# Loading each expert weight as two 1 MB transfers, awaited and released by halves

## The chip, the cores and the metric

The kernel runs on one core of one Trainium2 chip. The metric is the time of one execution on the device in microseconds (us), taken as the median of several runs. Before the change it is 1430.96 us (three runs, 1430.59 to 1434.89).

## What is computed

A decoder trunk of two layers over 256 tokens of width 1024, all in float32. Layer 0 mixes tokens by attention, layer 1 by a gated delta rule (GDN). After each mixer stands a layer norm, then a mixture of experts (MoE), then another layer norm:

```python
for layer in range(2):
    mix = attention_mixer(...) if layer % 2 == 0 else gdn_mixer(...)
    x = layer_norm(DEEPNORM_ALPHA * x + mix, ...)
    ffn = moe_ffn(x, router_w, router_bias, moe_w1[layer], moe_w3[layer], moe_w2[layer])
    x = layer_norm(DEEPNORM_ALPHA * x + ffn, ...)

def expert_block(xb, e):                      # inside moe_ffn
    hb = jax.nn.silu(xb @ w1[e]) * (xb @ w3[e])
    return hb @ w2[e]
```

Each token goes to the best 2 experts of one group of 8 out of 32. w1 and w3 of an expert are 1024 x 512, w2 is 512 x 1024: three matrices of 2 MB each, 6 MB per expert, 32 experts per layer, 384 MB for both layers.

## The kernel before, in words

The kernel loads the weights of every expert of both layers, whatever the routing is. The order of the work is written out by hand, engine by engine, with semaphores between them; there is no planner.

**The weight slots.** Nine slots of 2 MB each hold weights (`slot_tile`, L263): six in `ring` and three in a work area called `arena`. Attention and GDN use the ring slots for their own projection weights. In the MoE the nine slots hold three experts, and matrix m of expert n takes the slot `slot_moe(layer, 3 * n + m)` (L103): m = 0 is w1, 1 is w3, 2 is w2. The slots repeat every three experts.

**The loads.** All of them are issued by SyncE (SP) on its one hardware queue, in program order, by `load_expert` at L444 to L448. SP waits until a slot is free, then issues one transfer of 2 MB for it. For the first three experts of a layer `first_free` says what must be over (`free_for_moe0`, `free_for_moe1`: points of the attention or the GDN). From the fourth expert on, `freed` waits for PE to have finished the same matrix of the expert three before: `w1_used` for w1, `h_ps` for w3, `y_ps` for w2. Of w1 and w3 each of the 128 partitions gets one run of 16 KB, of w2 it gets two runs of 8 KB (`expert_parts`, `part`). After the last expert SP reads a flag (`load_more`), which sends nothing more when no expert has over 32 tokens, and then issues the GDN weights (`load_gdn`, L439, runs of 2 KB).

**TensorE** works through the experts in `experts` (L788; `turn` is one trip of three). For one expert: wait for w1, 64 matmul instructions at L803; wait for w3, 64 more; add the previous expert's output to the sum over experts (`scatter`, L784); transpose the gated product (L809); gather the next expert's tokens (`gather`, L763 and L766); wait for w2, 32 instructions at L817; transpose the next tokens (L774). The last instruction on a matrix raises the semaphore that frees its slot. ScalarE and VectorE run the gating between w3 and w2 and copy results out of PSUM. After the last expert PE runs one more `scatter`, and VectorE the layer norm.

**After `moe(0)`** PE goes on with the GDN; after `moe(1)` the final layer norm and the store of the output end the kernel.

Of the kernel before, what the change touches and what calls it, by code (L numbers as in the profile page):

```python
# [52 lines left out]
NE = 32  # L53
# [136 lines left out]
def build(nc, a, out):  # L190
    with ExitStack() as ctx:
# [3 lines left out]
        def sem(name):  # L195
            return ctx.enter_context(nc.semaphore(name))
# [118 lines left out]
        def gates_of(shape):  # L315
# [26 lines left out]
        ident_in, const_in, small_in, ln_in, gdn_in, out_done = (  # L342
            sem(n) for n in ("ident_in", "const_in", "small_in", "ln_in", "gdn_in", "out_done"))
        slot_full = [sem(f"slot_full{i}") for i in range(SLOTS)]
        x_half = [sem(f"x_half{t}") for t in range(NT)]
        first_in = [sem(f"first_in{i}") for i in range(2)]
        init = sem("init")
# [51 lines left out]
        def moe_sems(name):  # L399
            return [sem(f"{name}_{s}") for s in ("pick", "gathered", "xe", "gpt", "w1_used", "h_ps", "sig", "hm", "hT_ps",  # L400
                                                 "hT", "y_ps", "y", "own", "scattered")]

        fast_sems = moe_sems("moe")
        fast = [Moe(fast_sems), Moe(fast_sems, 1, NE)]
        more = [Moe(moe_sems("more0")), Moe(moe_sems("more1"))]
        more_full = [[sem(f"more{layer}_full{i}") for i in range(RING)] for layer in range(2)]

        block = ctx.enter_context(nc.Block())
# [21 lines left out]
        def _(sp):  # L430
            def part(m, slot):
                dst = slot_tile(slot)
                return dst.rearrange("p (h q) n -> p h (q n)", h=2) if m == 2 else dst

            def load_att(u, src):
                sp.dma_start(ring[:, slot_att(u)], src).then_inc(slot_full[slot_att(u)], 16)

# [3 lines left out]
            def load_experts(layer, first_free):  # L441
                s = fast[layer]

                def load_expert(e, c, wait):  # L444
                    for m, src in enumerate(expert_parts(layer, e)):
                        wait(m)
                        slot = slot_moe(layer, 3 * c + m)
                        sp.dma_start(part(m, slot), src).then_inc(slot_full[slot], 16)  # L448

                def freed(n):  # L450
                    def wait(m):
                        sp.wait_ge((s.w1_used, s.h_ps, s.y_ps)[m], n + (s.e + 1 - DEPTH))
                    return wait

                for n in range(DEPTH):
                    load_expert(n, n, lambda m: first_free(3 * n + m))
                for n in range(DEPTH, GROUP):
                    load_expert(n, n, freed(n))
                with sp.Fori(1, NE // GROUP) as i:
                    for c in range(GROUP):  # L460
                        load_expert(i * GROUP + c, c, freed(i * GROUP + c))
                for n in range(NE // GROUP * GROUP, NE):
                    load_expert(n, n % GROUP, freed(n))

            def load_more(layer):

                s = more[layer]
                sp.wait_ge(flag_sb, layer + 1)
                over = sp.value_load(flag[0:1, layer, 0:1])
                with sp.If(over > CAP):  # L470
                    sp.wait_ge(fast[layer].y_ps, NE + fast[layer].e)

                    def load_expert(n, c, again=True):
                        for m, src in enumerate(expert_parts(layer, n % NE)):
                            if again:
                                sp.wait_ge((s.w1_used, s.h_ps, s.y_ps)[m], n + (s.e + 1 - DEPTH))
                            sp.dma_start(part(m, 3 * c + m), src).then_inc(more_full[layer][2 * c + m // 2], 16)

                    for n in range(DEPTH):
                        load_expert(n, n, False)  # L480
                    with sp.Fori(1, (NIT - NE) // DEPTH) as i:
                        for c in range(DEPTH):
                            load_expert(i * DEPTH + c, c)
                    for n in range((NIT - NE) // DEPTH * DEPTH, NIT - NE):
                        load_expert(n, n % DEPTH)
                    sp.wait_ge(s.y_ps, NIT - NE)
                with sp.Else():
                    sp.nop()

# [102 lines left out]
        def _(pe):  # L592
# [192 lines left out]
                                  skip_group_check=not (stop and t == NT - 1), tile_position=(h * CAP, 0))  # L785
                return last

            def experts(s, steps, slot_of, full):  # L788

                def turn(i, cs, ends):  # L790
                    for c in cs:
                        n, b = i * GROUP + c, c % GROUP
                        ends_here = ends and c == cs[-1]
                        slots = [slot_of(3 * c + m) for m in range(3)]
                        filled = [full(i, c, m) for m in range(3)]
                        pe.wait_ge(s.xe, i * (2 * GROUP) + (2 * c + 2 + 2 * s.e))
                        pe.wait_ge(s.gpt, n + (2 + s.g))

                        for m in range(2):
                            pe.wait_ge(*filled[m])  # L800
                            for j in range(DJ):
                                for h in range(TILES):
                                    last = mm(psum[5][h * CAP:(h + 1) * CAP, m * FH:(m + 1) * FH], xeT[:, j],  # L803
                                              slot_tile(slots[m])[:, j, h // 2 * SEQ + h % 2:(h // 2 + 1) * SEQ:2],
                                              start=(j == 0), stop=(j == DJ - 1), tile_position=(0, h * CAP))
                            last.then_inc((s.w1_used, s.h_ps)[m], 1)
                        scatter(s, (b - 1) % GROUP, n + 1)
                        pe.wait_ge(s.hm, n + (1 + s.e))
                        transpose(psum[6][:, 0:P], hm, ident).then_inc(s.hT_ps, 1)  # L809
                        if not ends_here:  # L810
                            gather(s, (b + 1) % GROUP, n + 2)
                        pe.wait_ge(s.hT, n + (1 + s.e))
                        pe.wait_ge(*filled[2])
                        w2 = w2_view(slots[2])
                        for g in range(TILES):
                            for h in range(TILES):
                                last = mm(psum[7][h * CAP:(h + 1) * CAP, 0:Q], hT[:, g],  # L817
                                          w2[:, g // 2, g % 2, h * Q:(h + 1) * Q],
                                          start=(g == 0), stop=(g == TILES - 1), tile_position=(0, h * CAP))
                        last.then_inc(s.y_ps, 1)  # L820
                        if not ends_here:
                            turn_tokens(s, i * (2 * GROUP) + (2 * c + 3 + 2 * s.e))

                gather(s, 0, 1)
                turn_tokens(s, 1 + 2 * s.e)
                whole = (steps - 1) // GROUP
                with pe.Fori(0, whole) as i:
                    turn(i, range(GROUP), False)
                turn(whole, range(steps - whole * GROUP), True)
                scatter(s, (steps - 1) % GROUP, steps + 1, True).then_inc(s.scattered, 1)  # L830

            def moe(layer):
                router(layer)
                def full(i, c, m):
                    slot = slot_moe(layer, 3 * c + m)
                    return slot_full[slot], i * 16 + 16 * (MOE_BASE[layer][slot] + 1)

                def more_ready(i, c, m):
                    each = 16 if m == 2 else 32
                    return more_full[layer][2 * c + m // 2], i * each + each  # L840

                experts(fast[layer], NE, lambda u: slot_moe(layer, u), full)
                pe.wait_ge(flag_sb, layer + 1)
                over = pe.value_load(flag[0:1, layer, 0:1])
                with pe.If(over > CAP):
                    pe.wait_ge(more[layer].y, 1)
                    for h in range(TILES):
                        mm(psum[h][:], ident, y[:, :, h * Q:(h + 1) * Q], start=True, stop=False)
                    experts(more[layer], NIT - NE, lambda u: u, more_ready)
                with pe.Else():  # L850
                    pe.nop()
                pe.sem_inc(mix_ps, 4)
# [520 lines left out]
        def _(dve):  # L1373
# [268 lines left out]
            def moe(layer):  # L1642
# [4 lines left out]
                with dve.If(over > CAP):  # L1647
                    dve.wait_ge(fast[layer].scattered, 1 + fast[layer].runs)
                    experts(layer, more[layer], NIT - NE, NE)
                    dve.wait_ge(more[layer].scattered, 1)  # L1650
                with dve.Else():
                    dve.wait_ge(fast[layer].scattered, 1 + fast[layer].runs)
                layer_norm(1 + 2 * layer)
# [222 lines left out]
```

## Time and profile before

| what | value |
|---|---|
| median of 3 runs | 1430.96 us |
| the profiled execution's own time | 1432.51 us |
| its span, first to last instruction | 1430.6 us |
| mean granted TensorE clock | 0.945 |
| PE busy | 1161.7 us (81%) |
| DVE / ACT / POOL busy | 28% / 16% / 1% |
| DMA | 461.20 MB, mean 322 GB/s over the span |

Busy shares count instructions alone. The DMA share of a stretch is the mean over the core's 16 DMA engines of the time that their packets took; successive packets on an engine overlap by a few ns, so it can read a little over 1. A packet is one contiguous run, or the few bytes that raise a semaphore. Times are from the start of the span. "PE bank L803 <- DMA" in the waits means that a matmul at L803 stood still until a transfer landed.

### The profile page before, as it was taken

To read this page: it belongs to the slowest core of one execution; us is meant where nothing else is said; L and a number is where in the kernel's file an instruction comes from. 1 tells how busy PE (TensorE), PEld (TensorE's weight loads), DVE (VectorE), ACT (ScalarE), POOL (GpSimd) and SP (SyncE) were. 2 spreads that over 40 slices of the span, in tenths; PEclk is the share of its full clock that TensorE was granted. 3 is DMA by queue.
4 is the path that set the end of the run, shared out by engine and by line. 5 is a ranking of instruction groups with operands and counts; after the bars stand their busy time and mean duration, and the time that the engine had idled before them with its cause. 6 is when DMAs were issued, how large, how long until landed. Compare 5 with 4: busy or idle time off the path is not lost. (4 is left out here: it accounts for less than half of the span.)

```text
span 1430.6 us, 34064 instructions
## 1 busy us (share of the span) xinstructions
PE 1161.7 (81%) x14947; PEld 732.3 (51%) x14947; DVE 399.6 (28%) x1126; ACT 224.4 (16%) x589; POOL 14.4 (1%) x28
## 2 busy tenths in 40 slices
PE   8898779877777776759999899988987776777774
PEld 4444355544444444438778458445554444445442
DVE  1344512211111111133348744143211111111113
ACT  0123111100000010114433114110110010000001
POOL 0000100000000000010000000000000000000000
PEclk9999899989999999989999999998999999999998
DMA  9631599999999999973133341749999999999995
GB/s 361 253 118 59 211 412 425 429 423 429 424 427 427 426 427 424 427 302 118 59 118 118 118 146 62 281 198 379 424 429 425 425 426 426 427 426 428 425 424 209
DMA packets 63139, 461.20 MB, mean 322 GB/s; under 512 B 3824, under 2 KB 4000, under 8 KB 30320
## 3 DMA queue, kind: packets, MB, share of 16 engines
q1 hardware_dynamic: 61680, 455.92, 77.7%
q0 software_dynamic: 1408, 4.56, 0.8%
q8 instruction: 38, 0.62, 0.2%
q14 instruction: 13, 0.11, 0.0%
HBM read 459.41 MB, written 1.05 MB: 322 GB/s over the span
## 5 line engine op out<-in xcount | busy, mean ns | idle before, releaser
L803 PE MATMUL bank<-ring,arena 128*32 128x128 f32 x5568 | 191.4, 292 | 121.7 <-DMA ring<-in_moe_w 101.5
L803 PEld LDWEIGHTS bank<-ring,arena 128*32 128x32 f32 x5568 | 167.2, 114 | 142.7 <-DMA ring<-in_moe_w 82.5
L803 PE MATMUL bank<-arena 128*32 128x128 f32 x2624 | 103.2, 318 | 74.7 <-DMA arena<-in_moe_w 66.1
L1130 ACT ACTIVATE arena<-bank 128x256 f32<-128x256 f32 (+5 forms) x200 | 84.8, 431 | 368.6 <-PE bank L766 145.2
L1624 DVE SCALAR_TENSOR_TENSOR gated<-gated,bank 128x128 f32<-128x128 f32 x64 | 18.5, 288 | 428.4 <-ACT gated L1204 428.4
L763 PE MATMUL bank<-x,arena 128*32 128x256 f32 x1024 | 130.0, 637 | 4.5 <-DVEq L1585 4.5
L803 PEld LDWEIGHTS bank<-arena 128*32 128x32 f32 x2624 | 88.6, 125 | 85.8 <-DMA arena<-in_moe_w 79.3
L901 PE MATMUL bank<-xT,ring 128*128 128x256 f32 x512 | 115.2, 382 | 0.0
L901 PEld LDWEIGHTS bank<-xT,ring 128*128 128x128 f32 x512 | 96.6, 192 | 13.0 <-issue 0.4
L1204 ACT ACTIVATE gated<-bank 128x128 f32<-128x128 f32 x64 | 17.8, 278 | 466.7 <-PE bank L803 466.7
L784 PE MATMUL bank<-arena 32*128 32x256 f32 x1056 | 86.5, 444 | 4.8 <-issue 3.6
L639 PE MATMUL bank<-ring,xT 128*128 128x512 f32 x192 | 87.0, 606 | 2.3 <-DVEq L1466 2.0
L817 PE MATMUL bank<-ring,hT 128*32 128x256 f32 x1408 | 85.1, 382 | 3.3 <-DMA ring<-in_moe_w 3.3
L1630 DVE COPY arena<-bank 128x256 f32<-128x256 f32 x62 | 26.3, 425 | 185.0 <-PE bank L766 185.0
L784 PEld LDWEIGHTS bank<-arena 32*128 32x128 f32 x1056 | 54.2, 211 | 26.6 <-issue 21.4
L639 PEld LDWEIGHTS bank<-ring,xT 128*128 128x128 f32 x192 | 36.2, 194 | 44.6 <-issue 43.9
L971 PE MATMUL bank<-ring,xT 128*128 128x512 f32 x128 | 58.8, 613 | 0.0
L817 PEld LDWEIGHTS bank<-ring,hT 128*32 128x32 f32 x1408 | 41.6, 109 | 33.0 <-issue 10.7
L1100 PE MATMUL bank<-ring,arena 128*128 128x512 f32 x128 | 55.9, 594 | 1.6 <-ACT arena L1130 1.6
L763 PEld LDWEIGHTS bank<-x,arena 128*32 128x32 f32 x1024 | 29.4, 119 | 51.0 <-issue 38.9
L1633 DVE COPY arena<-bank 128x256 f32<-128x256 f32 x64 | 27.2, 425 | 99.1 <-PE bank L817 99.1
L1700 DVE SCALAR_TENSOR_TENSOR arena<-arena,cw 128x256 f32<-128x256 f32 x96 | 42.3, 482 | 40.2 <-ACT arena L1130 38.8
(229 smaller groups left out, 990.6 us busy)
## 6 DMA issues: line engine op xcount, KB each, us to landing
ring<-in_moe_w SPq DMA_DIRECT2D x131, 2048.0 KB, 40.5
arena<-in_moe_w SPq DMA_DIRECT2D x61, 2048.0 KB, 40.0
ring<-in_gdn_w_in SPq DMA_DIRECT2D x12, 2048.0 KB, 8.8
ring<-in_ab_w_in SPq DMA_DIRECT2D x5, 2048.0 KB, 23.1
ring<-in_gdn_w_out SPq DMA_DIRECT2D x4, 2048.0 KB, 8.6
ring<-in_ab_w_out SPq DMA_DIRECT2D x2, 2048.0 KB, 19.6
ring<-in_ab_w_in SPq DMA_DIRECT2D x2, 1024.0 KB, 8.2
x<-in_x SPq DMA_DIRECT2D x2, 512.0 KB, 4.4
```

What stands on the lines that cost most here:

```text
L639: last = mm(psum[4 + t][:], xT[:, j, t * P:(t + 1) * P], ring[:, slot_att(n), j], start=(j == 0), stop=(j == DJ - 1))
L763: mm(psum[4][h * CAP:(h + 1) * CAP, 0:Q].rearrange("p (c q) -> p c q", c=2), pick[:, b, t], by_j[:, h::TILES], start=(t == 0), stop=(t == ...
L784: last = mm(psum[h][:, t * Q:(t + 1) * Q], gpT[part, b, t], y_e[part], start=False, stop=stop and t == NT - 1, skip_group_check=not (stop ...
L803: last = mm(psum[5][h * CAP:(h + 1) * CAP, m * FH:(m + 1) * FH], xeT[:, j], slot_tile(slots[m])[:, j, h // 2 * SEQ + h % 2:(h // 2 + 1) * ...
L817: last = mm(psum[7][h * CAP:(h + 1) * CAP, 0:Q], hT[:, g], w2[:, g // 2, g % 2, h * Q:(h + 1) * Q], start=(g == 0), stop=(g == TILES - 1), ...
L901: last = mm(psum[n % 2][:, i * SEQ:(i + 1) * SEQ], ring[:, slot_gdn(n // 2), j, ch * P:(ch + 1) * P], xT[:, j], start=(j == 0), stop=(j == ...
L971: last = mm(psum[i % 2][:], xT[:, j, t * P:(t + 1) * P], ring[:, slot_gdn(8 + zz), j], start=(j == 0), stop=(j == DJ - 1))
L1100: last = mm(psum[GDN_OUT + 2 * h + t][:], goT[:, 8 * g + c, t * P:(t + 1) * P], ring[:, slot_gdn(12 + 2 * g + h), c], start=(g == 0 and c ...
L1130: return do(o, i, ACT.Copy, **kw)
L1630: o2.link(v.tensor_copy(gpT[:, (b + 1) % GROUP].rearrange("p t q -> p (t q)"), psum[5][:, 0:SEQ]))
L1633: o2.link(v.tensor_copy(y_e, psum[7][:, 0:Q]))
L1700: ins = v.scalar_tensor_tensor(out=cv[:, b, i], in0=xc[:, b, i, tap:tap + SEQ], scalar=cw[:, at:at + 1], in1=cv[:, b, i], op0=ALU.mult, op ...
```

## The change

Each expert matrix is loaded by two transfers of 1 MB instead of one of 2 MB. For w1 and w3 the first half is j = 0 to 3 of the eight contraction steps, so that each partition's run of 16 KB becomes two of 8 KB; for w2 the halves are the two runs of 8 KB that it already had. The second half has a semaphore of its own (`slot_full2`), and PE waits for each half just before its first matmul on it. PE also raises a semaphore after the first half of each matrix (`half_used`), and SP waits for that one before it issues the first half of the new contents, and for the old one before the second half. For the first three experts of a layer both halves are issued together after the old wait. The path for overflowing experts (`load_more`) keeps its 2 MB transfers and shares its semaphores between layers, to make room for the new ones; its waits are renumbered for that.

```diff
+            def halves(m, view):
+                return (view[:, 0], view[:, 1]) if m == 2 else (view[:, 0:DJ // 2], view[:, DJ // 2:])
...
                 def load_expert(e, c, wait):
                     for m, src in enumerate(expert_parts(layer, e)):
-                        wait(m)
                         slot = slot_moe(layer, 3 * c + m)
-                        sp.dma_start(part(m, slot), src).then_inc(slot_full[slot], 16)
+                        to, of = halves(m, part(m, slot)), halves(m, src)
+                        wait(m, 0)
+                        sp.dma_start(to[0], of[0]).then_inc(slot_full[slot], 16)
+                        wait(m, 1)
+                        sp.dma_start(to[1], of[1]).then_inc(slot_full2[slot], 16)
 
                 def freed(n):
-                    def wait(m):
-                        sp.wait_ge((s.w1_used, s.h_ps, s.y_ps)[m], n + (s.e + 1 - DEPTH))
+                    def wait(m, half):
+                        done = (s.w1_used, s.h_ps, s.y_ps)[m] if half else half_used[m]
+                        sp.wait_ge(done, n + (s.e + 1 - DEPTH))
                     return wait
...
                         for m in range(2):
-                            pe.wait_ge(*filled[m])
                             for j in range(DJ):
+                                if j % 4 == 0 and filled[m][j // 4]:
+                                    pe.wait_ge(*filled[m][j // 4])
                                 for h in range(TILES):
                                     last = mm(psum[5][h * CAP:(h + 1) * CAP, m * FH:(m + 1) * FH], xeT[:, j],
...
+                                if j == 3 and by_half:
+                                    last.then_inc(half_used[m], 1)
                             last.then_inc((s.w1_used, s.h_ps)[m], 1)
...
-                        pe.wait_ge(*filled[2])
                         w2 = w2_view(slots[2])
                         for g in range(TILES):
+                            if g % 2 == 0 and filled[2][g // 2]:
+                                pe.wait_ge(*filled[2][g // 2])
...
+                            if g == 1 and by_half:
+                                last.then_inc(half_used[2], 1)
                         last.then_inc(s.y_ps, 1)
```

## Rows read from the trace of the kernel before

**Rows 1.** The page: busy digits in 40 slices, PEclk the granted clock.

```profile
PE   8898779877777776759999899988987776777774
PEclk9999899989999999989999999998999999999998
DMA  9631599999999999973133341749999999999995
```

**Rows 2.** Busy by stretch: stretch, length, engines, PEclk, DMA share, GB/s.

```profile
200.00:600.00 400.00, 308.83 (x5632) 194.06 (x5624) 66.75 (x230) 37.84 (x114) 0.00 (x0) 0.94 1.01 426
990.00:1400.00 410.00, 315.09 (x5816) 199.48 (x5810) 68.16 (x235) 39.23 (x119) 0.00 (x0) 0.95 1.01 426
```

**Rows 3.** Waits of the whole span: who for whom, us, times, longest.

```profile
PE bank L803 <- DMA ring<-in_moe_w: 101.5, 46, 2.8
PE bank L803 <- DMA arena<-in_moe_w: 66.1, 25, 2.9
```

**Rows 4.** PE in order of time, one expert whose weights were there already.

```profile
230.25 3.90 PE L803 MATMUL bank<-ring,arena 128*32 128x128 f32 x128 [0.66 <-ACT arena L1130]
240.69 3.89 PE L803 MATMUL bank<-arena 128*32 128x128 f32 x128 [0.64 <-ACT arena L1130]
```

**Rows 5.** SP's DMA issues in order of time, both layers' starts.

```profile
159.21 0.81 SPq L448 DMA_DIRECT2D ring<-in_moe_w  x2
...
183.60 20.71 SPq L448 DMA_DIRECT2D ring<-in_moe_w  x6
...
979.50 10.90 SPq L448 DMA_DIRECT2D ring<-in_moe_w  x4
```

**Rows 6.** DMA packets of 200 to 600 us (MoE of layer 0).

```profile
DMA packets 15184, 170.42 MB, mean 426 GB/s; under 512 B 1301, under 2 KB 1301, under 8 KB 1301
```

**Rows 7.** DMA packets of 26 to 50 us (attention weights, runs of 2 KB).

```profile
DMA packets 4611, 9.27 MB, mean 386 GB/s; under 512 B 91, under 2 KB 92, under 8 KB 4610
```

**Rows 8.** PE in order of time, end of the MoE of layer 0.

```profile
611.23 2.04 PE L803 MATMUL bank<-ring,arena 128*32 128x128 f32 x64 [1.94 <-DMA ring<-in_moe_w]
616.05 2.03 PE L803 MATMUL bank<-ring,arena 128*32 128x128 f32 x64 [2.79 <-DMA ring<-in_moe_w]
618.01 1.15 PE L784 MATMUL bank<-arena 32*128 32x256 f32 x16
619.13 0.33 PE L809 MATMUL bank<-const,gated 128*128 128x128 f32 x1
621.14 1.93 PE L817 MATMUL bank<-ring,hT 128*32 128x256 f32 x32 [1.68 <-DMA ring<-in_moe_w]
```

**Rows 9.** ACT in the same stretch: the copy of hT.

```profile
619.49 0.28 ACT L1130 ACTIVATE hT<-bank 128x128 f32<-128x128 f32 x1 [1.06 <-PE bank L809]
```

**Rows 10.** PE, end of the MoE of layer 1.

```profile
1407.19 2.04 PE L803 MATMUL bank<-arena 128*32 128x128 f32 x64 [2.75 <-DMA arena<-in_moe_w]
1412.18 1.94 PE L817 MATMUL bank<-ring,hT 128*32 128x256 f32 x32 [1.58 <-DMA ring<-in_moe_w]
```

**Rows 11.** PE, first expert of layer 1.

```profile
975.64 5.56 PE L803 MATMUL bank<-ring,arena 128*32 128x128 f32 x128 [0.65 <-ACT arena L1130]
984.83 1.93 PE L817 MATMUL bank<-ring,hT 128*32 128x256 f32 x32
```

**Rows 12.** Stretches at the start of layer 1's MoE, columns of group 2.

```profile
970.00:975.00 5.00, 3.36 (x20) 1.13 (x20) 2.02 (x9) 0.38 (x1) 0.00 (x0) 0.50 1.01 422
975.00:978.00 3.00, 2.35 (x45) 2.19 (x49) 0.54 (x3) 0.38 (x1) 0.00 (x0) 0.50 0.84 350
978.00:981.00 3.00, 3.00 (x89) 2.83 (x80) 0.00 (x0) 0.00 (x0) 0.00 (x0) 0.78 0.44 76
981.00:984.00 3.00, 3.00 (x41) 1.32 (x33) 0.57 (x2) 0.56 (x2) 0.00 (x0) 1.00 0.80 322
```

**Rows 13.** L448 from 200 to 620 us: duration ns min/median/max.

```profile
L448 SPq DMA_DIRECT2D ring<-in_moe_w x55: 332/3852/6844, 203.9 to 579.8; - x55
```

**Rows 14.** L448 over the whole span: issue to landing.

```profile
DMA to landing us min/median/max: 7.8/40.4/42.2
```

More of the change, by code:

```diff
@@ L344, in build @@
         slot_full = [sem(f"slot_full{i}") for i in range(SLOTS)]
+        slot_full2 = [sem(f"slot_full2_{i}") for i in range(SLOTS)]
+        half_used = [sem(f"half_used{m}") for m in range(3)]
         x_half = [sem(f"x_half{t}") for t in range(NT)]
@@ L404, in build @@
         fast = [Moe(fast_sems), Moe(fast_sems, 1, NE)]
-        more = [Moe(moe_sems("more0")), Moe(moe_sems("more1"))]
+        more = [Moe(moe_sems("more")), Moe(fast_sems, 2, 2 * NE)]
         more_full = [[sem(f"more{layer}_full{i}") for i in range(RING)] for layer in range(2)]
@@ L445, in load_expert @@
                     for m, src in enumerate(expert_parts(layer, e)):
-                        wait(m)
                         slot = slot_moe(layer, 3 * c + m)
-                        sp.dma_start(part(m, slot), src).then_inc(slot_full[slot], 16)
+                        to, of = halves(m, part(m, slot)), halves(m, src)
[3 more added lines that the diff above has]
+                        sp.dma_start(to[1], of[1]).then_inc(slot_full2[slot], 16)
                 def freed(n):
-                    def wait(m):
-                        sp.wait_ge((s.w1_used, s.h_ps, s.y_ps)[m], n + (s.e + 1 - DEPTH))
+                    def wait(m, half):
+                        done = (s.w1_used, s.h_ps, s.y_ps)[m] if half else half_used[m]
+                        sp.wait_ge(done, n + (s.e + 1 - DEPTH))
                     return wait
                 for n in range(DEPTH):
-                    load_expert(n, n, lambda m: first_free(3 * n + m))
+                    load_expert(n, n, lambda m, half: None if half else first_free(3 * n + m))
                 for n in range(DEPTH, GROUP):
@@ L485, in load_more @@
                         load_expert(n, n % DEPTH)
-                    sp.wait_ge(s.y_ps, NIT - NE)
+                    sp.wait_ge(s.y_ps, NIT - NE + s.e)
                 with sp.Else():
@@ L786, in scatter, with experts @@
                 return last
-            def experts(s, steps, slot_of, full):
+            def experts(s, steps, slot_of, full, by_half=False):
                 def turn(i, cs, ends):
@@ L794, in turn @@
                         slots = [slot_of(3 * c + m) for m in range(3)]
-                        filled = [full(i, c, m) for m in range(3)]
+                        filled = [[full(i, c, m, half) for half in range(2)] for m in range(3)]
                         pe.wait_ge(s.xe, i * (2 * GROUP) + (2 * c + 2 + 2 * s.e))
@@ L833, in moe, with full, more_ready @@
                 router(layer)
-                def full(i, c, m):
+                def full(i, c, m, half):
                     slot = slot_moe(layer, 3 * c + m)
+                    if half:
+                        return slot_full2[slot], i * 16 + 16 * (layer * (NE * 3 // SLOTS + (slot < NE * 3 % SLOTS)) + 1)
                     return slot_full[slot], i * 16 + 16 * (MOE_BASE[layer][slot] + 1)
-                def more_ready(i, c, m):
+                def more_ready(i, c, m, half):
+                    if half:
+                        return None
                     each = 16 if m == 2 else 32
                     return more_full[layer][2 * c + m // 2], i * each + each
-                experts(fast[layer], NE, lambda u: slot_moe(layer, u), full)
+                experts(fast[layer], NE, lambda u: slot_moe(layer, u), full, True)
                 pe.wait_ge(flag_sb, layer + 1)
@@ L845, in moe @@
                 with pe.If(over > CAP):
-                    pe.wait_ge(more[layer].y, 1)
+                    pe.wait_ge(more[layer].y, 1 + more[layer].g)
                     for h in range(TILES):
@@ L1649, in moe @@
                     experts(layer, more[layer], NIT - NE, NE)
-                    dve.wait_ge(more[layer].scattered, 1)
+                    dve.wait_ge(more[layer].scattered, 1 + more[layer].runs)
                 with dve.Else():
```

## The prediction

> **What bounds the kernel now.** I read the page's digits first [rows 1]: the DMA engines stand at 9 in two long blocks, slices 5 to 16 and 27 to 38 (the first is 0), which are the two MoE stages, and far lower in the attention and the GDN, where PE reads 7 to 9. In the table by stretch [rows 2] the DMA share is 1.01 at 426 GB/s in both MoE stages, while PE is busy 308.8 of 400 us. The waits say the same from the other side [rows 3]: 168 us in which a w1 or w3 matmul stood still for a weight transfer, 71 times, never over 2.9 us at once. An expert whose weights are there already takes PE 240.69 − 230.25 = 10.44 us [rows 4]; 6.29 MB at 426 GB/s take 14.77. So about 895 of the 1431 us (159 to 621, 979 to 1412) are a stream of weights that never pauses, and what the stream takes is what counts: when it starts, how long it is, and how much work is left behind its last byte. The rest is bound by PE and its helpers and has no term in this change.
>
> **Is there anything that an earlier release can win inside the stream?** No. SP issues a transfer a median of 40.4 us before it lands [rows 14], which at 14.77 / 3 = 4.92 us each is eight transfers in the queue, and SP's own issue instruction takes a median of 3.85 us and at best 0.33 [rows 13]: it is the queue that holds SP up, not the slots. Releasing a slot 1 us sooner makes SP wait at the queue instead. What releasing or awaiting by halves can move is only the two ends of each stream.
>
> **Start of the layer 0 stream.** It starts at 159.21 when the attention is over [rows 5], a wait that the change leaves as it is. Its first nine slots keep it fed: five transfers, 25 us of work from 159.2, last until about 185, and the first release is issued at 183.60 [rows 5]. Slice 5 of the page is full [rows 1]. Gain 0.
>
> **Start of the layer 1 stream.** Here there is a hole. The prefetched slots run out at about 978 (share 1.01 until 975, then 0.84 and 0.44 at 76 GB/s) [rows 12], and the first refill is issued at 979.50 [rows 5], when PE has done w1 of the first expert. PE starts that at 975.64 [rows 11]; the granted clock there is 0.50, the lower of the two levels (1.2 GHz) [rows 12], so w1 takes 979.4 − 975.6 = 3.7 us and its first half half of that. The refill goes out 1.85 us sooner, at 977.6. It does not run into a new hole: its 1 MB takes 2.5 us, the second half goes out at 979.5 and w3's first at about 980.5. By the time w2 is to be refilled (first half released in the middle of the matmuls at 984.83 [rows 11]) four halves are queued. I take 1.8 us; bounds 0 (if the hole is a latency that stays) and 3, the whole hole from 978 to about 981.
>
> **End of both streams.** In layer 0 w3 lands just before 616.05, its 64 instructions take 2.03 us, h is complete at 618.0, and hT is copied at 619.49 + 0.28 = 619.8; w2 lands just before 621.14 and its 32 instructions take 1.93 us [rows 8, 9]. After the change half of w3's matmuls is done before its last half lands, so hT is ready at 618.8; half of w2 lands 2.5 us before the rest, at 618.6, so that its 16 instructions run from 618.8 to 619.8; and behind the last byte stand 0.97 us of matmuls in place of 1.93. Layer 1 ends the same way, w3 at 1407.19 and w2 at 1412.18 for 1.94 us [rows 10]. Gain 2 × 0.97 = 1.9 us; bounds 0 and 2 × 1.93. The DVE copy, scatter and layer norm behind it are as long as before, and they move with it.
>
> **What the halves cost the stream.** Each of the 128 runs of 16 KB of w1 and w3 becomes two of 8 KB; w2's runs stay at 8 KB. The price of one more packet isn't a row, but two streams with other packet sizes give it. Per DMA engine, 26 to 50 us: 16 × 24 us over 4611 − 92 = 4519 data packets of 2 KB is 85 ns each, at 386 GB/s [rows 7]. 200 to 600 us: 16 × 400 us over 15184 − 1301 = 13883 data packets of 170.42 MB / 13883 = 12275 bytes is 461 ns each [rows 6]. The line through both is 9.6 ns a packet plus 0.0367 ns a byte. The 2 KB stretch also carries a little other traffic, so 9.6 is rather high than low. Check: an expert now is 2 × 8 packets of 16 KB and 16 of 8 KB on each engine, 32 × 9.6 ns + 393 KB × 0.0367 = 14.75 us against 14.77 measured.
>
> How many transfers are in the streams: of layer 0's 96 all from the fifth on, 92, of which 61 are w1 or w3; of layer 1's all from the tenth on, 87, of which 58. 119 transfers × 8 further packets on each engine × 9.6 ns = 9.1 us. Each split transfer also adds one small packet on each engine that raises its semaphore (the 1301 packets under 512 B for 81 transfers [rows 6]); 179 of these at nothing to 9.6 ns are 0 to 1.7 us, I take 0.9. Together 10.0 us. From below the bound is 0, if a half of a 16 KB run is as cheap as half of its time. From above it is what the matmuls' starts suggest on a naive reading: w1 to w3 is 616.05 − 611.23 = 4.82 us, w3 to w2 621.14 − 616.05 = 5.09 [rows 8], and if the whole 0.27 us were w2's shorter runs, 119 × 0.27 = 32 us. I stay near the fit, since a matmul's start also holds what stands between the landing and it, and this differs from place to place; the fit goes over thousands of packets.
>
> **What I cost at nothing.** PE's three further waits and three further increments an expert stand beside 4.3 us of idle PE an expert; without that cover they'd matter in the first three experts only, which the stream hides too. SP issues six times an expert instead of three: 6 × 0.33 = 2.0 us and three waits in 14.9 us. Behind each of SP's new waits are the loads of the following matrices, and behind them the GDN weights; with the queue's 40 us of work ahead, nobody waits for those. If the queue holds a number of transfers and not of bytes, eight halves are still 20 us, against a longest wait of SP's for PE of some 6 us in the middle of a stream (10.44 us for a whole expert). The overflow path is not run.
>
> **The sum**, on the profiled execution: 1432.51 + 10.0 − 1.8 − 1.9 = 1438.8 us. The median of the runs is 1.55 us below the profiled one, so the forecast is 1437.3 us, 0.44% slower. What a measurement can tell from no change is 0.3%, 4.3 us: 1426.7 to 1435.3 is "the same".
>
> The Trainium skill speaks against small transfers: "DMA: Bandwidth & Descriptors", section "Measured (HBM→SBUF, 128 partitions, SWDGE, issued from GpSimd)", wants at least 1 MiB a DMA, and the section "Anatomy of one DMA — SWDGE (gpsimd) path" fits 2.0 us plus the bytes at 436 GB/s. By that fit an expert would be 20.4 us in 2 MB transfers and 26.4 in halves, an estimate for a path that this kernel's loads don't use. The trace disagrees already for 2 MB: 4.92 us each, less than the fit by 1.9.
>
> **The rivals.**
> 1. *Splitting a run is free* (not slower). The 9.6 ns are a property of the 2 KB stream's scattered rows and not of a packet, so only the ends move: 1430.96 − 3.7 = 1427.3 us. For it: the check of 14.75 against 14.77 doesn't test the two sizes apart. Against it: one line fits two stages with quite different addresses. The break-even is 3.7 us / 952 = 3.9 ns a packet, less than half of what the fit gives; above it the kernel is slower. Chance 0.09, on either side of 1426.7 about equally.
> 2. *Half runs cost more than the line says*, because reads of 8 KB at a step of 16 KB, or the first packets after a transfer's end, go slower: up to the naive 0.27 us a transfer, 1430.96 + 32 − 3.7 = 1459; halfway 1444. For it: w3 to w2 in [rows 8]. Against: 2 KB runs at a wider step keep 386 GB/s [rows 7]. Chance 0.09.
> 3. *The clock.* PE's work comes in smaller pieces; if it stands at the lower level behind the last byte of a stream, about 3 us of matmuls there take 6. Instead of the gain of 1.9 the ends then lose 2 × 2: 1441. Against: busy time per expert is the same, and the mean granted clock is 0.94 and 0.95 now [rows 2]. Chance 0.06.
> 4. *The fixed cost of a transfer shows.* A lone transfer takes at least 7.8 us from issue to landing [rows 14], 2.9 over its 4.9 in the stream. Paid by all 179 further transfers: 1431 + 519 = 1950 us. It needs a queue that runs dry between two transfers, and the share of 1.01 [rows 2] with eight waiting excludes that nearly. Chance 0.01. The fit of the skill's page above is this rival's rule; the trace bears it out only for a lone transfer.
>
> **How the numbers follow.** The forecast's own case has 0.75, with a range of 1433 to 1441: 0.62 slower by over 0.3%, 0.13 within. Rival 1 gives 0.05 faster and 0.04 same, rival 2 0.09 slower, rival 3 0.05 slower and 0.01 same, rival 4 0.01 slower. Sum: faster 0.05, same 0.18, slower 0.77. The range for 8 in 10 is 1432 to 1444: it leaves out rival 1, most of rival 2 and rival 4.
>
> **What would show it.** After the change: in 200 to 600 us about 168.8 MB at 422 GB/s, in some 20,600 data packets of 8 KB in place of 13,883, with the share still at 1.01; an expert's period of 14.93 us in place of 14.77; the MoE stretch of layer 0 longer by 5 us, that of layer 1 by as much minus 1.8; the first refill of layer 1 issued 1.85 us after the start of its first w1 and not 3.86; 16 and not 32 instructions at L817 behind the last landing of each layer, and 32 of w3. I am wrong if the rate in the streams stays at 426 GB/s (rival 1), if it is below 420 (rival 2), if the share falls below 1 (rival 4), or if the time between the last landing and the layer norm doesn't shrink by 1 us.

## The result, and the profile after

| | before | after |
|---|---|---|
| median, 20 runs each | 1432.4 us (1427.93 to 1439.01) | 1438.11 us (1434.59 to 1442.76) |
| ratio to before, 95% interval | | 1.0039 (1.0025 to 1.0053) |
| profiled execution | 1432.51 us | 1442.76 us |
| mean granted clock | 0.945 | 0.933 |

The kernel became 5.6 us slower by the ratio (0.39%, interval 0.25 to 0.53, or 3.6 to 7.6 us); 6.3 us were forecast. The profiled execution after is the slowest of its 20. Its stretch from the last w2 matmul of layer 0 to the first w1 matmul of layer 1, which holds the GDN and which the change does not touch, took 358.9 us at a granted clock of 0.94; a second trace of the same kernel has 352.4 at 0.96, and two traces of the kernel before have 352.6 and 355.4, both at 0.96. These differences are as large as the effect, so below I compare streams and ends, not spans.

Lines of the page and the two MoE stretches, columns as in [rows 2]:

```profile
PE   8898889877777787859999899988997777777774
PEclk9999899989989899989999999999999999999987
DMA  9631599999999999983124322649999999999995
...
200.00:600.00 400.00, 315.61 (x5581) 188.20 (x5573) 66.18 (x228) 37.95 (x115) 0.00 (x0) 0.92 1.01 422
990.00:1400.00 410.00, 324.93 (x5834) 195.27 (x5830) 69.53 (x240) 39.35 (x119) 0.00 (x0) 0.93 1.01 422
```

The streams are as full as in [rows 1, 2], the share is 1.01 again, but they move 422 GB/s and not 426. The packets of 200 to 600 us show what changed:

```profile
DMA packets 23165, 168.72 MB, mean 422 GB/s; under 512 B 2574, under 2 KB 2574, under 8 KB 2574
```

20,591 data packets of 8 KB stand where 13,883 of 12.3 KB on the average stood [rows 6]. The ends of the two streams on PE, layer 0 and then layer 1:

```profile
618.16 1.14 PE L813 MATMUL bank<-ring,arena 128*32 128x128 f32 x32 [1.36 <-DMA ring<-in_moe_w]
620.64 1.13 PE L813 MATMUL bank<-ring,arena 128*32 128x128 f32 x32 [1.35 <-DMA ring<-in_moe_w]
621.70 1.15 PE L793 MATMUL bank<-arena 32*128 32x256 f32 x16
...
623.51 1.07 PE L830 MATMUL bank<-ring,hT 128*32 128x256 f32 x16 [0.37 <-ACT hT L1149]
625.64 1.07 PE L830 MATMUL bank<-ring,hT 128*32 128x256 f32 x16 [1.06 <-DMA ring<-in_moe_w]
...
1421.63 1.07 PE L830 MATMUL bank<-ring,hT 128*32 128x256 f32 x16 [0.37 <-ACT hT L1149]
1423.68 1.07 PE L830 MATMUL bank<-ring,hT 128*32 128x256 f32 x16 [0.98 <-DMA ring<-in_moe_w]
```

Where 64 and 32 instructions stood behind one landing [rows 8, 10] there are groups of 32 and 16, each with its own wait, and 16 behind the last. The 16 take 1.07 us and the 32 took 1.93. And the start of layer 1's stream, PE and then SP:

```profile
985.59 3.89 PE L813 MATMUL bank<-ring,arena 128*32 128x128 f32 x128 [0.65 <-ACT arena L1149]
...
986.94 0.34 SPq L454 DMA_DIRECT2D ring<-in_moe_w  x1
987.83 0.34 SPq L456 DMA_DIRECT2D ring<-in_moe_w  x1
988.62 0.33 SPq L454 DMA_DIRECT2D ring<-in_moe_w  x1
```

The first refill goes out 1.35 us after the first w1 began and not 3.86 [rows 5, 11]. But the granted clock is full here and was at half there; a second trace of the kernel before has it full, and its refill goes out after 2.26 us:

```profile
978.59 3.90 PE L803 MATMUL bank<-ring,arena 128*32 128x128 f32 x128 [0.65 <-ACT arena L1130]
...
980.85 10.85 SPq L448 DMA_DIRECT2D ring<-in_moe_w  x4
```

At the same clock the release by halves brings the refill 0.9 us forward.

### The profile page after: what moved, and what is told of

Same layout as the page of the kernel before. It is cut to its first block and busy times, and to the rows that moved or that the text cites. A ratio compares the mean times of both kernels' runs of the same rounds, so it can differ in the third digit from the quotient of the medians.

```text
span 1441.0 us, 34546 instructions
## 1 busy us (share of the span) xinstructions
PE 1187.3 (82%) x14947; PEld 725.1 (50%) x14947; DVE 399.5 (28%) x1126; ACT 224.1 (16%) x589; POOL 14.4 (1%) x28
## 5 line engine op out<-in xcount | busy, mean ns | idle before, releaser
L813 PE MATMUL bank<-ring,arena 128*32 128x128 f32 x5568 | 200.7, 292 | 114.9 <-DMA ring<-in_moe_w 80.4
L813 PEld LDWEIGHTS bank<-ring,arena 128*32 128x32 f32 x5568 | 161.3, 114 | 150.5 <-DMA ring<-in_moe_w 111.0
L813 PEld LDWEIGHTS bank<-arena 128*32 128x32 f32 x2624 | 80.0, 119 | 87.2 <-DMA arena<-in_moe_w 73.8
L793 PE MATMUL bank<-arena 32*128 32x256 f32 x1056 | 93.7, 474 | 4.5 <-issue 3.3
L1223 ACT ACTIVATE gated<-bank 128x128 f32<-128x128 f32 x64 | 17.7, 277 | 461.6 <-PE bank L813 461.6
L793 PEld LDWEIGHTS bank<-arena 32*128 32x128 f32 x1056 | 57.9, 224 | 27.0 <-issue 20.8
L1719 DVE SCALAR_TENSOR_TENSOR arena<-arena,cw 128x256 f32<-128x256 f32 x96 | 42.3, 482 | 41.8 <-ACT arena L1149 40.4
```

The lines of the kernel that those rows point to most:

```text
L793: last = mm(psum[h][:, t * Q:(t + 1) * Q], gpT[part, b, t], y_e[part], start=False, stop=stop and t == NT - 1, skip_group_check=not (stop ...
L1719: ins = v.scalar_tensor_tensor(out=cv[:, b, i], in0=xc[:, b, i, tap:tap + SEQ], scalar=cw[:, at:at + 1], in1=cv[:, b, i], op0=ALU.mult, op ...
```

## The experiments

Each kernel's time is compared with the kernel before, measured beside it on the same chip: 4 to 20 executions of each, and 10 to 23 of the kernel before. That kernel's second trace has a single execution. "Stream 0" is the time from the first issue after the attention to the last landing of layer 0's weights; "stream 1" runs from PE's first w1 matmul of layer 1 to the last landing; "behind" is the time from each layer's last landing to the end of its w2 matmuls. "Period" is the time per expert, from landings on the same slot. These four are worked out from the landings and starts in one trace of each kernel.

| kernel | ratio (95%) | stream 0 | period | stream 1 | behind |
|---|---|---|---|---|---|
| before | 1 | 461.8 | 14.76 | 436.4 | 2.07, 2.07 |
| before, again | | 461.4 | 14.76 | 434.5 * | 2.07, 2.07 |
| changed | 1.0039 (1.0025, 1.0053) | 465.5 | 14.91 | 438.1 * | 1.11, 1.11 |
| changed, again | 1.0031 (1.0015, 1.0047) | 465.7 | 14.91 | 439.6 | 1.67, 1.11 |
| 8 KB runs, 2 MB transfers | 1.0064 (1.0047, 1.0082) | 465.7 | 14.91 | 440.3 | 2.25, 2.07 |
| split transfers alone | 1.0048 (1.0033, 1.0063) | 465.5 | 14.91 | 440.4 | 2.38, 2.07 |
| release by halves alone | 1.0038 (1.0024, 1.0052) | 465.6 | 14.92 | 440.5 | 2.44, 2.46 |
| await by halves alone | 1.0047 (1.0030, 1.0064) | 465.8 | 14.91 | 438.6 * | 1.11, 1.11 |
| halves of w2 alone | 0.9985 (0.9973, 0.9998) | 461.6 | 14.77 | 434.7 * | 1.11, 1.11 |
| halves of the last experts alone | 0.9984 (0.9971, 0.9997) | 461.5 | 14.76 | 436.6 | 3.39, 1.11 |
| w2 in runs of 16 KB | 1.0123 (1.0104, 1.0141) | 458.6 | 14.69 | 434.7 | 13.24, 14.79 |

\* the first expert of layer 1 ran at full granted clock (its w1 and w3 in 3.9 us, not 5.5); compare these among themselves. For halves of the last experts, the period is that of the experts before the last two, which are loaded as in the kernel before. In the last row the matmuls of w1 and w3 take twice as long, so its stream 1 and "behind" stand by themselves.

Of the 2.07 us behind a landing 1.93 are the 32 instructions; of the 1.11 us 1.07 are the 16. In the rows above the last, each value over 2.07 or 1.11 stands where the granted clock had fallen to 0.5 shortly before the last landing, so that w3's matmuls and the scatter took longer and hT came late.

**The kernel before once more**, unchanged.

> The kernel before once more, for a second trace beside the first: stream of layer 0, from its first issue at the end of the attention to its last landing, 461.8 us as in the first trace, stream of layer 1, from the first refill's issue to the last landing, 432.5. All theories agree.

Stream 0 is within 0.4 us. Its stream 1 from PE's first w1 is 1.9 us shorter; for 1.6 of these the first refill goes out sooner, after 2.26 us and not 3.86, since w1 runs at full clock. From the first refill's issue it is 432.2 us, against 432.5.

**The changed kernel once more**, unchanged.

> The changed kernel once more, beside the others on the same chip: 0.39% slower than before as measured, 5.6 us. The stretch from 200 to 600 us at 422 GB/s. Packet theory and rival agree here; it is the yardstick for the run with split transfers alone.

1.0031; the two measurements agree within their intervals.

**Runs of 8 KB in transfers of 2 MB.** This takes the packets alone, with neither more transfers nor halves (excerpt; w3 as w1).

```diff
-            w1 = a["moe_w1"][...].rearrange("a (p j) f -> (a p) j f", j=DJ)
+            w1 = a["moe_w1"][...].rearrange("a (h p j) f -> (a p) h (j f)", h=2, j=DJ // 2)
...
-                    by_j = x[:, t].rearrange("p (q j) -> p j q", j=DJ)
+                    by_j = x[:, t].rearrange("p (c q j) -> p j c q", c=2, j=TILES)
```

> The kernel before, still with transfers of 2 MB and waits and releases by whole matrices, but w1 and w3 come in two runs of 8 KB per partition (rows h*512 + p*4 + j, and the gather picks the tokens' columns to match). Packet theory: 119 transfers in the streams times 8 more packets on each engine times 9.6 ns = 9.1 us slower than before, 0.64%, nothing given back at the ends; 422 to 423 GB/s in 200 to 600 us, against 426. Rival, the cost comes with the number of transfers or their semaphores and a split run is free: no difference, 426 GB/s. If the queue in front of the engines holds a number of packets, issue to landing falls from 40 us towards 27; if it holds transfers, it stays at 40.

Measured 0.64% (0.47 to 0.82), as expected. The stretch from 200 to 600 us:

```profile
DMA packets 21874, 168.72 MB, mean 422 GB/s; under 512 B 1281, under 2 KB 1281, under 8 KB 1281
```

The same 422 GB/s and, with 20,593, the changed kernel's number of data packets, with half its small ones, and a period of 14.91 us: the whole slowdown of the stream is there without one more transfer. The rival in which a split run is free is out. Issue to landing fell to a median of 32.7 us, less far than expected.

**Split transfers alone**: as changed, but released and awaited whole.

```diff
                         wait(m, 0)
                         sp.dma_start(to[0], of[0]).then_inc(slot_full[slot], 16)
-                        wait(m, 1)
                         sp.dma_start(to[1], of[1]).then_inc(slot_full2[slot], 16)
...
+                            for half in range(2):
+                                if filled[m][half]:
+                                    pe.wait_ge(*filled[m][half])
```

> The changed kernel with its transfers of 1 MB, but a slot is released and awaited whole: both halves are issued after the old wait, and PE waits for both before its first matmul. Packet theory: packets 9.1 us and 179 semaphore packets 0.9 us slower than before, 10.0 us or 0.70%, so 3.7 us slower than the changed kernel, which gains 1.9 us at the ends of the two streams and 1.8 at the start of the second. Rival, halves gain nothing: equal to the changed kernel, 5.6 us over before. Behind the last landing of each layer 32 instructions of w2, 1.93 us.

The excerpt leaves out the removal of `half_used` and the same wait for both halves of w2. The ratio is 1.0048 (0.33% to 0.63%), so the 0.70% expected was too much; the sum below says where. Against the run before it, twice the transfers change neither a stream nor the period by what I can see. Against the changed kernel (1.0039 and 1.0031) the ratios' intervals overlap, so the times do not show the 3.7 us between the two that were expected. In layer 1, behind its last landing stand all 32 instructions again:

```profile
1418.69 1.93 PE L829 MATMUL bank<-ring,hT 128*32 128x256 f32 x32 [1.52 <-DMA ring<-in_moe_w]
```

**Release by halves alone** and **await by halves alone**: each is the changed kernel with one half of its edit undone, the waits of PE in the first, the early releases in the second.

> The changed kernel with its releases by halves, but PE waits for both halves of a matrix before its first matmul on it. Halves theory: the two ends give nothing (1.93 us of w2 matmuls behind the last landing of each layer), the start of layer 1's stream keeps what it gives: the first refill is issued when half of the first w1 is used, 1.0 us sooner than with whole releases where the granted clock is full there, up to 1.8 where it is at half. So about 1.9 us slower than the changed kernel and 1 to 1.8 faster than with split transfers alone. Rival, the release does nothing because a fixed latency of the first transfer fills the hole: equal to split transfers alone, 0.48% over before.

> The changed kernel with PE waiting by halves, but both halves of a slot issued together after the old wait for the whole matrix. Halves theory: 1.9 us from the two ends (0.98 us of matmuls behind the last landing), nothing at the start: between the changed kernel (1.0031 to 1.0039) and split transfers alone (1.0048), near 1.0035; its stream of layer 1 from first refill to last landing is 436.5 us like that of split transfers alone. Rival, all that the changed kernel gets back comes from the releases: equal to split transfers alone.

The times, 1.0038 and 1.0047, come out in the other order than expected, but their intervals overlap widely and the traces are clearer. Awaiting has the ends (1.11 and 1.11) and nothing else. Releasing has its first refill out early, at half clock 2.16 us after the first w1 matmul against 3.87:

```profile
977.76 5.43 PE L814 MATMUL bank<-ring,arena 128*32 128x128 f32 x128 [0.75 <-ACT arena L1151]
...
979.92 0.34 SPq L454 DMA_DIRECT2D ring<-in_moe_w  x1
981.57 0.34 SPq L456 DMA_DIRECT2D ring<-in_moe_w  x1
```

but its stream 1 is 440.5 us, as long as with split transfers alone. The third half to land does so 13.8 us after PE's start against 14.8, so 1 us was won there; by the end the slowest DMA engine is 3.7 us behind the fastest, against 2.3, and the gain is gone. That this spread ate it is a guess; no run varies it.

**Halves of w2 alone**, whose runs were 8 KB already; w1 and w3 whole as before.

```diff
+                        if m < 2:
+                            wait(m, 0)
+                            sp.dma_start(part(m, slot), src).then_inc(slot_full[slot], 16)
+                            continue
```

> The changed kernel with w1 and w3 loaded, awaited and released whole again, in runs of 16 KB; w2 alone goes by halves, whose runs were 8 KB already. Packet theory: 60 more semaphore packets, 0.4 us, and the same 1.9 us at the two ends, since hT is ready 1.3 us before the last half lands as it is: 1.5 us faster than before, 0.1%, and 426 GB/s. Rival, any half costs 3 to 4 us a layer by its transfers: 1 to 2 us slower than before.

**Halves for the last two experts of each layer alone**, transfers and waits.

```diff
-                    load_expert(n, n % GROUP, freed(n))
+                    load_expert(n, n % GROUP, freed(n), True)
```

> The kernel before, with halves (transfers and waits, not releases) for the last two experts of each layer alone; all others in transfers of 2 MB with 16 KB runs. Packet theory: 8 w1 and w3 transfers times 8 packets times 9 ns are 0.6 us, the two ends give back 1.9: 1.3 us faster than before, 0.1%, within the noise of the times; in the trace 16 and not 32 instructions of w2 behind the last landing of each layer. Rival, the ends give nothing: 0.6 us slower.

The excerpt leaves out the waits. Both beat the kernel before, by 0.15% (0.02 to 0.27) and 0.16% (0.03 to 0.29), intervals that leave out no change only just; against the changed kernel's ratios that is about 0.5% less. 200 to 600 us with halves of w2 alone:

```profile
200.00:600.00 400.00, 302.37 (x5636) 190.28 (x5629) 66.72 (x230) 37.84 (x114) 0.00 (x0) 0.95 1.01 426
...
DMA packets 15624, 170.41 MB, mean 426 GB/s; under 512 B 1738, under 2 KB 1738, under 8 KB 1738
```

437 small packets more than in [rows 6] and the same 426 GB/s: one more transfer an expert adds 5 ns to the period, no more than the traces of one kernel differ by. So it isn't the halves that cost, nor their number; it is the shorter runs. Of the 2.2 us that halves of w2 gained, 1.9 are the two ends. The rest fits a detail that was in nobody's sum: from the end of layer 1's w2 matmuls to the end of the kernel it is 16.2 us in this and in every kernel built from the changed one, and 16.5 in the two traces of the kernel before; the cause is open.

Halves of the last experts show what the clock does at an end. Layer 0, PE and then a stretch:

```profile
615.12 1.94 PE L815 MATMUL bank<-ring,arena 128*32 128x128 f32 x32 [0.86 <-DMA ring<-in_moe_w]
616.99 2.09 PE L794 MATMUL bank<-arena 32*128 32x256 f32 x16
619.01 0.48 PE L821 MATMUL bank<-const,gated 128*128 128x128 f32 x1
619.85 3.60 PE L830 MATMUL bank<-ring,hT 128*32 128x256 f32 x32 [0.37 <-ACT hT L1147]
...
613.00:623.00 10.00, 8.78 (x109) 4.94 (x101) 0.57 (x2) 1.84 (x3) 0.00 (x0) 0.50 1.02 402
```

PE worked through w2 without a wait for its second half, but at a granted clock of 0.50: 3.60 us, and 3.39 of them behind the last landing at 620.06. In this trace layer 0's end lost 1.3 us against whole waits instead of gaining 1.0.

**w2 in runs of 16 KB**, the packet cost taken away where the kernel before still had it:

```diff
-            w2 = a["moe_w2"][...].rearrange("a (h p c) n -> (a p) h (c n)", h=2, c=2)
+            w2 = a["moe_w2"][...].rearrange("a (p c) n -> (a p) (c n)", c=TILES)
...
-                                              slot_tile(slots[m])[:, j, h // 2 * SEQ + h % 2:(h // 2 + 1) * SEQ:2],
+                                              slot_tile(slots[m])[:, j, h::TILES],
```

> The kernel before, with w2 in one run of 16 KB per partition too (rows 4p to 4p+3), and the w1 and w3 columns read with a step of 4 elements in place of 2 to match. Packet theory: 60 w2 transfers in the streams (31 and 29) times 8 fewer packets on each engine times 9.6 ns = 4.6 us faster than before, 0.32%, 428 GB/s in 200 to 600 us. Rival, a run's length is free between 8 and 16 KB: no difference, 426 GB/s. Should the wider step slow the matmuls at L803 (292 ns now), PE has 4.3 us an expert to hide it, save behind the last w3, where it shows in full.

1.0123 (1.0104 to 1.0141), 1.2% slower. By stretch, the matmuls of w1 and w3 over the span (busy, mean ns, idle before), and 32 of them in order of time:

```profile
200.00:600.00 400.00, 381.78 (x5579) 216.01 (x5569) 65.46 (x226) 37.27 (x113) 0.00 (x0) 1.00 1.01 428
990.00:1400.00 410.00, 390.92 (x5714) 223.59 (x5709) 67.26 (x232) 38.33 (x116) 0.00 (x0) 1.00 1.01 427
...
L803 PE MATMUL bank<-ring,arena 128*32 128x128 f32 x5568 | 331.0, 409 | 34.7 <-ACT arena L1130 34.7
L803 PE MATMUL bank<-arena 128*32 128x128 f32 x2624 | 157.9, 409 | 6.5 <-ACT arena L1130 6.5
...
299.64 2.05 PE L803 MATMUL bank<-arena 128*32 128x128 f32 x32
```

The stream did what was expected, 428 GB/s in layer 0, with a period of 14.69 us in place of 14.76: 8 packets fewer per engine and expert give back 9 ns each. This is the price of a packet once more, from the other side. But reading the columns with a step of 4 floats instead of 2 doubles the matmuls: 32 of them take 2.05 us, where 64 took 2.03 [rows 8]. PE is busy 382 of 400 us and has fallen behind the stream; behind the last landing of layer 1 its w1, w3 and w2 matmuls still run for 14.8 us. The expectation named slower matmuls, but took the 4.3 us of cover in every expert to be enough.

**Transfers cut by partitions**, 64 and 64, so that runs stay at 16 KB:

```diff
-                return (view[:, 0], view[:, 1]) if m == 2 else (view[:, 0:DJ // 2], view[:, DJ // 2:])
+                return view[0:P // 2], view[P // 2:P]
```

> Each weight in two transfers of 1 MB, but cut by partitions (64 and 64) instead of by contraction steps, so that w1 and w3 keep their runs of 16 KB; both issued after the old wait, both awaited before the first matmul. Packet theory: only 179 more semaphore packets, of about 6 ns each by their spacing in the trace: 1 us, not to be told from before; 426 GB/s in 200 to 600 us. Rival, the number of transfers costs: as slow as the kernel with split transfers alone (0.48%, 7 us), 422 GB/s.

The transfers are issued and awaited as with split transfers alone. The six executions took 2215.76 to 2314.94 us, median 2281.94, 1.59 times the kernel before (the two fastest 1.55 times); both theories missed. From 200 to 600 us:

```profile
200.00:600.00 400.00, 206.59 (x3007) 139.91 (x3011) 35.67 (x124) 20.02 (x61) 0.00 (x0) 0.72 1.01 221
```

The engines are as busy as ever and move half as much. This says nothing on the number of transfers; halves of w2 alone and split transfers alone settled that.

## Why the prediction was right

**Bound and cover.** Right. The share stayed at 1.01 and the stream's length set the time. PE's busy time in 200 to 600 us rose from 308.8 to 315.6 us, and its idle time beside the stream covered that.

**Runs of 8 KB, +10.0 us.** The right mechanism, a little over-sized. A packet's price was put at 9.6 ns from the line through two stages. The prediction's check of that line (14.75 against 14.77) was no test, since the line goes through the same stretch. The runs of 8 KB in 2 MB transfers are one: 14.91 − 14.76 = 0.15 us a period over 16 packets is 9.4 ns, and w2 in runs of 16 KB gives 9. The trace of the kernel before had the price in it too, as both sizes stand in one stream: in 200 to 600 us 6964 packets of 8 KB took a mean of 314.0 ns and 6919 of 16 KB 615.1 ns. Two of the smaller are 12.9 ns longer than one of the larger, less some 3.6 ns by which successive packets overlap there (all packets together took 6455 us, on 16 engines in 400 us): about 9.3 ns, an estimate. The small packets, put at 0.9 us in all, cost too little to see. Over whole streams the sum came to less: stream 0 grew by 4.0 us (465.6 against 461.6, means of four and two traces), and stream 1, from its first refill, from 432.4 to 436.5 with 8 KB runs and with split transfers, by 4.1. That is 8.1 us where 119 × 8 × 9.4 ns gives 9.0. I can't place the 0.9; the lead of the fastest DMA engine over the slowest at the last landing, 2.1 to 3.1 us in all traces but that of release alone, moves by as much.

**Ends, −1.9 us.** Right: 2.07 us from the last landing to the end of w2 became 1.11 in both layers, 2 × 0.96, and awaiting alone gives it, as does w2 alone. One qualification, which rival 3 had in it: in the second trace of the changed kernel layer 0 has 1.67 us. The granted clock stood at 0.51 from 617 to 624 us, the scatter ahead took 2.09 us and not 1.15, and hT came after w2.

**Start of layer 1, −1.8 us.** This term was mis-sized. The refill did go out sooner, by 0.9 us at full clock and by 1.7 at half, but at like clocks stream 1 is shorter than with whole releases by 0.7 us in one pair (439.6, again, against 440.4), 0.5 in another (438.1 against 438.6), and by nothing with release alone. These are single traces, and two of the kernel before differ by 0.4 us in stream 0, so 0 to 0.7 is all that can be said. I had taken a sooner issue for a sooner end of the stream. In part the hole is a first transfer's latency: in the changed kernel the prefetched halves still land until 989.0, the refill issued at 986.9 lands at 992.9, and 1.4 us of hole remain, as many as with awaiting alone (1.5), where the refill goes out 0.9 us later; only the next hole, 0.6 us there, has shrunk to 0.2. The size also hangs on the granted clock at that place, which was at half in the trace that I read and full in others of the same kernel.

**The sum.** 8.1 − 1.9 − 0.5 = 5.7 us, against 5.6 and, again, 4.4 measured and 6.3 forecast. The over-sized cost and the over-sized gain partly cancelled, which is luck. The agreement to 0.1 us is luck too: each measurement is good to some 2 us, and the sum leaves out the 0.3 us behind w2 in layer 1 and what the clock does in the GDN.

**The rivals.** That a split run is free (1) fell with the 8 KB runs. Costlier half runs (2) too: the naive 0.27 us a transfer would have made the period 15.3. The clock (3) came in part. It stood at half just before an end in several traces, also of kernels that await whole, where it cost 0.2 to 0.4 us; 0.56 us in the changed kernel, and 2.3 with halves of the last experts (3.39 against 1.11). Its own sum was wrong in the prediction: without the gain of 1.9 and with a loss of 4 the forecast becomes 1443.2 us, not 1441. Over the whole execution the mean granted clock was 0.932 to 0.935 in the three traces in which PE awaits all matrices by halves, against 0.942 to 0.946 in those that await whole (0.976 with w2 in runs of 16 KB, where PE is busier). Two of these three, and no other, have some 359 us ahead of layer 1's MoE; all others have 352 to 356. Whether awaiting by halves brings that on is not shown. Were it in most executions, the changed kernel's time would stand several us above the sum of its streams and ends, and it does not. The fixed cost of a transfer (4) does not show: 179 more transfers leave the period at 14.91 us.

## What to carry to other kernels

Where DMA engines are busy all the time, count packets before cutting a transfer: here the cut was free along an edge that the runs already had (w2's halves), and cost 9.4 ns per further packet on each engine where it shortened runs from 16 to 8 KB. Unbroken runs are not enough, though: the cut across partitions kept them and halved the rate. Finer waits and releases paid only at the ends of the stream, so do it for the last matrices alone, and read the granted clock there before counting on it. The price of a packet can be had before any change, from the rates of two stages whose packets differ.

## What had not been expected of the hardware

- Transfers to 64 partitions moved 221 GB/s at a DMA share of 1.01, those to 128 partitions 426. The Trainium skill has a possible reason, in "DMA: Bandwidth & Descriptors", section "The descriptor swizzle": in a transfer to 128 partitions, partitions 0 to 63 are written through the eight even ports and the rest through the eight odd ones. By its section "Where 436 GB/s comes from", sixteen ports give 435 GB/s, so eight would carry 218, an estimate; the trace's 221 is 1.5% above it. Which port a packet used no run here shows.
- A moving operand of float32 read with a step of 4 elements took 64 ns an instruction of 128 columns (2.05 us for 32), with a step of 2 it took 32 (2.03 us for 64), both at full granted clock.
- Issue to landing, with the queue full, had a median of 40.4 us with 9, 9 and 17 packets per matrix on each engine, 32.7 with 17 each in one transfer (8 KB runs), and 26.6 in two of 9 (split transfers alone). The last two:

```profile
DMA to landing us min/median/max: 7.4/32.7/38.3
...
DMA to landing us min/median/max: 4.9/26.6/29.9
```

  At periods of 14.76, 14.91 and 14.91 us that is 96, 112 and 96 packets, and 8, 7 and 11 transfers. What fills the queue looks more like a number of packets than of transfers or bytes; no run was made for it.
- The stretch from the last w2 matmul of layer 0 to the first w1 matmul of layer 1 took 352.4 and 358.9 us in two traces of the changed kernel, at a granted clock of 0.96 and 0.94, and 352.6 and 355.4 in two of the kernel before, both at 0.96; so the clock is not all of it. The spread is more than the effect studied here.
